# Output projection of the last attention: by token halves of both column tiles between the heads

## The reference, cut to what matters

```python
for blk in range(t // Q_BLOCK):                    # two blocks of 128 queries
    s = einsum('bqhd,bkhd->bhqk', qb, kb) * scale  # 8 heads x 2 sub-heads
    p = softmax(where(allowed, s + bias, -inf))
    attn = p[:, :, 0] - lam_full * p[:, :, 1]
    o = einsum('bhqk,bkhe->bqhe', attn, vb)
    o = o * rsqrt(mean(o * o) + SUBLN_EPS) * subln_g * (1.0 - lambda_init)
h = concatenate(outs, axis=1) @ w_o                # 256 x 1024 by 1024 x 1024
x = layer_norm(ALPHA * x + h, ...)
x = layer_norm(ALPHA * x + square(relu(x @ mlp_w1)) @ mlp_w2, ...)
```

## Time and profile before

| | |
|---|---|
| timed executions, median (lowest to highest) | 1381.98 us (1381.8 to 1383.23) |
| span of the profiled execution | 1382.5 us; the page gives no time for it outside the span |
| PE busy | 1346.9 us, 97% |
| DVE busy | 864.3 us, 63% |
| ACT busy | 673.8 us, 49% |
| stage of the change: from the last k-projection to the MLP's first tile | about 1147 to 1202 us |

### The profile page before, as it was taken

The page is one execution under the profiler, slowest core; times in us unless marked ns, Lnnn a source line. Parts: engine busy times, 40 slices in busy tenths (PEclk is TensorE's granted clock), DMA queues, the critical chain, the costliest instruction groups (busy, mean ns, idle before and its releaser), DMA issues.

```text
span 1382.5 us, 26707 instructions
## 1 busy us (share of the span) xinstructions
PE 1346.9 (97%) x11635; PEld 1195.1 (86%) x11635; DVE 864.3 (63%) x1388; ACT 673.8 (49%) x1202; POOL 87.7 (6%) x104
## 2 busy tenths in 40 slices
PE   8999999999999999999999999999999998999997
PEld 6888998988867889998799999799987896799996
DVE  6786655573395655556685666856467556856565
ACT  6775544552384545442651224445443468545452
POOL 3000400000060000000000430000000000000000
PEclk9999999999999999999999999999999999999999
DMA  9345555453302555554233000655545451555550
GB/s 350 124 182 198 183 183 183 183 198 123 147 38 68 193 189 188 196 191 151 105 140 123 4 5 34 240 200 184 183 183 183 153 183 62 179 193 190 199 184 31
DMA packets 17635, 215.18 MB, mean 156 GB/s; under 512 B 1976, under 2 KB 2144, under 8 KB 4848
## 3 DMA queue, kind: packets, MB, share of 16 engines
q1 hardware_dynamic: 15888, 205.54, 40.3%
q0 software_dynamic: 1632, 7.94, 1.6%
HBM read 212.41 MB, written 1.06 MB: 154 GB/s over the span
## 4 chain that ended last, share of the span: by engine, by line
PE 84%; DVE 9%; ACT 4%; DMA 1%; issue 1%; SPq 0%; DVEq 0%; ACTq 0%
PE psum L665 24%; PE psum L471 11%; PE psum L472 11%; PE psum L473 11%; PE psum L1008 3%; DVE w_low L1862 3%; PE psum L1089 2%; PE psum L569 1%; PE psum L1141 1%; ACT w_high L1342 1%; PE psum L540 1%; PE psum L565 1%; PE psum L541 1%; PE psum L542 1%; DMA ring<-weights 1%; PE psum L561 1%
## 5 line engine op out<-in xcount | busy, mean ns | idle before, releaser
L1862 DVE TENSOR_TENSOR w_low<-ring,w_high 128x1024 fp32r<-128x1024 f32 x368 | 437.0, 1222 | 231.7 <-ACT w_high L1342 231.7
L1342 ACT ACTIVATE w_high<-ring 128x1024 fp32r<-128x1024 f32 x368 | 368.6, 1047 | 175.9 <-PE psum L665 155.4
L471 PE MATMUL psum<-act_split,w_high 128*128 128x256 f32 x1312 | 381.7, 291 | 3.7 <-DVE w_low L1862 3.6
L472 PE MATMUL psum<-act_split,w_high 128*128 128x256 f32 x1312 | 372.5, 284 | 0.0
L473 PE MATMUL psum<-act_split,w_low 128*128 128x256 f32 x1312 | 372.3, 284 | 0.0
L665 PE MATMUL psum<-w_high,up_split 128*128 128x512 f32 x1024 | 287.6, 391 | 0.8 <-DVE up_split L2010 0.8
L471 PEld LDWEIGHTS psum<-act_split,w_high 128*128 128x128 f32 x1312 | 252.6, 193 | 11.6 <-DVE w_low L1862 4.7
L472 PEld LDWEIGHTS psum<-act_split,w_high 128*128 128x128 f32 x1312 | 253.0, 193 | 2.6 <-issue 1.4
L473 PEld LDWEIGHTS psum<-act_split,w_low 128*128 128x128 f32 x1312 | 252.9, 193 | 0.0
L665 PEld LDWEIGHTS psum<-w_high,up_split 128*128 128x128 f32 x1024 | 190.4, 188 | 40.5 <-issue 2.7
L665 PE MATMUL psum<-w_low,up_split 128*128 128x512 f32 x512 | 163.1, 390 | 0.0
(11 more groups left out here) (338 smaller groups left out, 1661.3 us busy)
## 6 DMA issues: line engine op xcount, KB each, us to landing
ring<-weights SPq DMA_DIRECT2D x95, 2048.0 KB, 7.8
work<-rows POOLq DMA_DIRECT2D x4, 1024.0 KB, 5.0
ring<-weights SPq DMA_DIRECT2D x4, 512.0 KB, 8.5
work<-rows POOLq DMA_DIRECT2D x4, 512.0 KB, 5.6
x<-x_in SPq DMA_DIRECT2D x2, 512.0 KB, 4.4
work<-t_bias POOLq DMA_DIRECT2D x1, 1024.0 KB, 8.9
out<-x SPq DMA_DIRECT2D x4, 256.0 KB, 2.0
con<-consts SPq DMA_DIRECT2D x1, 687.0 KB, 21.6
```

Source lines behind the costliest of these rows:

```text
L471: mm(out, w_hi, x_hi, start=start, stop=False)
L472: mm(out, w_hi, x_lo, start=False, stop=False)
L1342: A(high[:, HIGH_SLOT[name], f], ring[:, n % RING, f], ACT.Copy).then_inc(weights_high, 1)
L1862: V.tensor_tensor(low[:, n % RING, f], ring[:, n % RING, f], high[:, HIGH_SLOT[name], f].bitcast(f32), ALU.subtract).then_inc(weights_spli ...
```

## The change: token half 0 of both tiles between the heads

The number of instructions stays the same on every engine; the order changes on PE, and with it the turn list and DVE's order.

- `out_chunk(k, n)` becomes `out_half(k, n, th)`, a half-chunk. Chunks 0 to 3 of tile 0 are still done for both token halves, before the scores of head 7.
- After the scores of head 7 come (k,n,th) = (4,0,0) and (0,1,0) in place of chunk 4 of tile 0; (0,1,0) opens bank 2. After the values of head 6: (5,0,0), (1,1,0), (2,1,0), (3,1,0). After the values of head 7: (4,1,0), (5,1,0), (6,0,0), (4,0,1).
- After the last output transposes: (5,0,1), (6,0,1), (7,0,0), (0,1,1), (1,1,1), (6,1,0), (7,1,0), (7,0,1), then (2,1,1) to (6,1,1), `norm(7, 0)`, (7,1,1).
- Accumulators are filled in the order (0,0), (0,1), (1,0), (1,1); the turn list says so, with the banks unchanged.
- DVE's `norm(7)` loses the `add_in` (1,0) ahead of quarter 0; the existing line `if order[2] == (1, 0)` now does it after quarter 1, ahead of the low parts of token half 0. The other norms keep their order.

```diff
-_mixer_turns(3)
+_norm_turns(7, [(0, 0), (0, 1), (1, 0), (1, 1)], banks={(0, 0): 0, (1, 0): 1, (0, 1): 2, (1, 1): 3})
...
-            out_chunk(4)
+            out_half(4, 0, 0)
+            out_half(0, 1, 0)
             da_transposes(6)
             out_transposes(5)
             da_values(6)
-            out_chunk(5)
-
-            out_chunk(0, 1)
+            out_half(5, 0, 0)
+            out_half(1, 1, 0)
+            out_half(2, 1, 0)
+            out_half(3, 1, 0)
             da_transposes(7)
             out_transposes(6)
             da_values(7)
-            out_chunk(1, 1)
-            out_chunk(6)
+            out_half(4, 1, 0)
+            out_half(5, 1, 0)
+            out_half(6, 0, 0)
+            out_half(4, 0, 1)
             out_transposes(7)
-            out_chunk(2, 1)
-            out_chunk(7)
-            project_out("da_o", 7, act_split, halves=(1,), ks=range(3, NC))
+            out_half(5, 0, 1)
+            out_half(6, 0, 1)
+            out_half(7, 0, 0)
+            out_half(0, 1, 1)
+            out_half(1, 1, 1)
+            out_half(6, 1, 0)
+            out_half(7, 1, 0)
+            out_half(7, 0, 1)
+            for k in range(2, NC):
+                if k == NC - 1:
+                    norm(7, 0)
+                out_half(k, 1, 1)
             mlp(3, 2)
...
                 add_in(i, *order[0])
-                if i % 2:
-                    add_in(i, *order[1])
+                if order[1] == (1, 0):
+                    add_in(i, 1, 0)
                 quarter(0)
```

More of the change, by code:

```diff
@@ L99, with _norm_turns @@
 ACC, TR = {}, {}
-def _norm_turns(i, order, transposes=True):
+def _norm_turns(i, order, transposes=True, banks=None):
     ACC[i], TR[i] = {}, {}
@@ L108, in _norm_turns @@
                 TR[i][(0, n)] = len(BANK) - 1
-        _turns(("acc", i, half), 1, j)
+        _turns(("acc", i, half), 1, banks[half] if banks else j)
         ACC[i][half] = len(BANK) - 1
@@ L1258, in early_heads, with out_half @@
                     da_values(step // 16 - 1)
-            def out_chunk(k, n=0):
+            def out_half(k, n, th):
                 w_hi, w_lo = split_tile(f"da_o{n}")
@@ L1264, in out_chunk @@
                 read_out(pe, TURN[("dot", k)])
[L1265 to L1275, removed]
+                f, t = slice(k * 512, k * 512 + 512), slice(P * th, P * th + P)
+                q = ACC[7][(th, n)]
+                if k == 0:
+                    open_bank(q)
+                for i, (a, w) in enumerate(((0, w_hi), (0, w_lo), (1, w_hi))):
+                    last = mm(bank(q), act_split[:, k, a, t], w[:, f], start=(k == 0 and i == 0),
+                              stop=(k == NC - 1 and i == 2))
+                if k == NC - 1:
+                    last.then_inc(bank_filled, 1)
+            def out_chunk(k):
+                out_half(k, 0, 0)
+                out_half(k, 0, 1)
             project("da_q0", TURN[("da_q", 0)], act_split, beside=beside_queries, second=TURN[("da_q", 1)])
```

## The result

The changed kernel takes 1385.55 us (median of 15 runs, 1383.1 to 1387.25); the kernel before, run beside it 15 times, takes 1383.23 (1380.92 to 1385.18). The ratio is 1.0018, with a 95% interval of 1.0011 to 1.0026: slower by 2.5 us, between 1.5 and 3.6 (the medians themselves are 2.3 apart). The profiled execution of the changed kernel took 1385.41 us with a span of 1383.6, so about 1.8 us lie outside the span.

A forecast was written before the change was run, and what follows sets the result against it. DVE's chain was taken to bound the stage, with PE never pausing behind it. +0.6 (bank 2) + 3.2 (wait for ACT's copy) - 1.68 (closed holes) = +2.1 us on the median 1381.98 gave 1384.1 us, range 1382.0 to 1385.7.

The forecast's parts named there:

- Bank 2, +0.6: After head 7's scores, the half-chunk opening bank 2 waits for DVE's last read: +0.5 and +0.1 us, not absorbed.
- the term of 0.1: At the opening of bank 2, the first matmul after a wait takes 0.34 us to the next instead of 0.23.
- ScalarE's copy starts 12 matmuls later: At the projection's end, the up3_0 copy waits for accumulator (1,0), now filled at the 24th matmul; DVE idles 3.2 us.
- Part 3: End of the projection: ACT's up3_0 copy comes later, and DVE, executing in order, gets 3.2 us of new idle time.
- The holes that close, -1.68: DVE's idle stretches in the stage, 0.24, 1.24 and 0.20 us, close; 1.68 us is the most it can save.
- the sum of +2.1: Whole kernel: +0.6 for bank 2, +3.2 for DVE's wait on ACT's copy, -1.68 for closed holes.
- Parts 2, 4 and 5: Half-chunk swaps between heads cost 0; add_in (1,0) fills DVE's hole after token half 0's norm; down3_0's later load is covered.
- The clock: PE's first idle stretch, 3.3 us, most likely slows the clock off the path; the second, 1.5 us, priced at 0.
- How the numbers follow: Chances for the whole kernel: within 0.2% 0.72, slower by over 0.2% 0.24, faster by over 0.2% 0.04.
- the first rival: Quarter 0 of up3_0 is not late and the holes close: about -0.9 us, 1381.1 us; chance 0.10.
- the third rival: The clock falls in PE's second gap too, ahead of token half 1's transposes: +3.5, 1385.5 us; chance 0.18.
- The second (bank 2 free): Opening bank 2 early costs nothing and the rest stands: +1.5, 1383.5 us; chance 0.12.

The follow-up runs named there:

- e2: The changed kernel with bank 2 opened after the values of head 6 instead of right after the scores of head 7; ratio 1.0006 to the kernel before.
- e1: The changed kernel with VectorE's add_in of accumulator (0,1) ahead of quarter 0 of up3_0 instead of behind it; ratio 1.0013 to the kernel before.
- e4: The changed kernel with bank 2 opened late, accumulators filled (0,0), (1,0), (0,1), (1,1), and VectorE's order as before the change; 1382.1 us, ratio 0.9988.
- e3: The changed kernel with eight idle 128x512 matmuls on TensorE ahead of token half 0's transposes; ratio 1.0018 to the kernel before.
- e5: e4 with token half 1's two low parts ahead of the first two quarters of down3_0 on VectorE; ratio 0.9995 to the kernel before.

## Why the prediction was right or wrong

The mechanism and the size of the sum were right; the step from the sum to the forecast, no change, was wrong.

- *Bank 2, +0.6*: right. 0.60 in the distance from scores to transposes, 0.60 back in the stage of e2. One row was misread on the way: the 0.34 us from 1165.26 to 1165.60, taken for the cost of the first matmul after a wait, stand behind score matmuls and no wait. Behind the real wait of the changed kernel the first matmul took 1166.02 - 1165.71 = 0.31 us to the next, so the term of 0.1 held.
- *ScalarE's copy starts 12 matmuls later and VectorE idles 3.2 us behind (0,0)*: right, 3.15 us. e1 showed that it is the quarter and gave 1.14 us of the delay back. It also showed a second thing on the same hook, the root behind the copies, which Part 3 passed over.
- *The holes that close, -1.68, and the sum of +2.1*: the stage is 1.98 us longer, 0.60 ahead of VectorE's chain and 1.38 on it, where the sum had 0.6 and 3.2 - 1.68 = 1.5. e4 gives the other end of the same account: with both causes out 1.89 us come back against the kernel before, not the 4.5 that TensorE loses there. e3 shows directly that TensorE has room in its first wait.
- *Parts 2, 4 and 5 at nothing*: nothing shows against them. No wait is left ahead of (1,0) or (1,1), ScalarE starts to copy `down3_0` at 1194.83 without a wait, straight behind the norm's root, and TensorE's stretch behind the stage is as busy as before.
- *The clock*: I held a fall in the first gap for most likely and named the gap of 1.56 us as one that did no harm. In the changed kernel's profile it was the other way round: 1.00 after 3.11 us of idling, and 0.50 after the 1.56 us ahead of the last heads. Since the first gap was followed by full speed, TensorE came to the second one earlier and waited 2.37 us there, not 1.5; with a fall, in e2, it waited 0.72. In the stage the fall costs nothing: with the clock falling (e2) or not, the end is where VectorE sets it.
- *Where it failed* is "How the numbers follow". From a sum of +2.1 us it gave 0.72 to "within 0.2%" and 0.24 to "slower", because 0.2% was taken as what a measurement can tell from no change. The ratio is 1.0018 with an interval that ends at 1.0011 on the lower side. The kernel is slower, by less than that bound but clear of no change. The terms of the sum could be traced to rows and only the first rival had the other sign, so the direction, slower by 0.15%, should have been the forecast; calling it no change threw away what the sum said. The other fault there is the base of the absolute number: 1381.98 was the median of three runs, and 15 runs of the same kernel gave 1383.23. Of the 1.45 us between 1384.1 and 1385.55, 1.25 is that, 0.2 the rest. The measured time lies inside the stated range (1382.0 to 1385.7) by 0.15 us, and that is luck: the range reached so far only to take in the third rival, which did not occur.

Rivals: the first (1381.1) and the third (1385.5, the clock falling in the second gap) did not occur: no fall follows the second gap, and the profile of the third would have shown matmuls 0.43 apart there. The third's time lies nearest to the measured one by accident of the base. The second (bank 2 free) is refuted by the wait of 0.38 us.

What stays open: the timed difference is 2.5 us (1.5 to 3.6) and the stage accounts for 1.98. The interval holds it, but single runs of one kernel spread over 4 us and the stage starts anywhere between 1161.95 and 1165.93 us in the seven profiles. Part of that spread goes with TensorE's granted clock. Among the 35 executions of the kernel before that were timed beside e1 to e4, the three with a mean granted clock of 0.994 have a median of 1381.9 us and the eleven with 0.990 one of 1384.18. The profiles have their falls ahead of the stage in different places: e4's, whose stage starts earliest, is the only one without a fall behind the wait of 1.99 us near 81 us. That the falls cause the spread was not tried.

## What to carry to other kernels

When an accumulator is finished earlier or later, list everything that uses its "full" as a signal. Here the same event also freed the slot for the next weight's copy, and the engine that needed the copy had it queued ahead of the sum that had been brought forward. And before one reorders the engine that waits, it pays to add up the work of the engine that it waits for: TensorE lost 4.5 us, but VectorE had only 1.7 us of holes, and that is about what the best order tried gave (1.89).

## What the runs showed of the hardware

- In these profiles the length of an idle stretch did not decide whether the clock fell. Ahead of the transposes of token half 0, TensorE was idle for 2.18 us and the clock fell in the kernel before; after 1.95 us in e1 (0.50 from 1190 to 1192 us) and 3.10 us in e2 it fell; after 3.11 us in the changed kernel it did not.
- The same stretch of instructions, ahead of every edit, came out both ways. TensorE idles for 1.56 us ahead of the last heads in all seven profiles; then follow seven small matmuls and a wait of 0.58 us. The clock stayed at 1.00 before, in e1, e2 and e3, and was at 0.50 behind it in the changed kernel (rows below), in e4 (1149 to 1151 us) and in e5 (1152 to 1154 us). Behind the wait of 1.99 us near 81 us it fell in six profiles and stayed at 1.00 in e4.

```profile
1148.10 0.66 PE L1248 MATMUL psum<-con,work 128*128 128x128 f32 x4 [1.56 <-ACT work L1795]
...
1149.66 0.79 PE L1239 MATMUL psum<-work 128*128 128x128 f32 x2 [0.58 <-ACT work L1778]
...
1150.00:1152.00 2.00, 2.00 (x12) 1.78 (x13) 1.04 (x3) 2.00 (x10) 0.00 (x0) 0.50 1.00 422
```

- The Trainium skill ("TensorE: Matmul & The Clock Gate", section "HAM oscillation — how this bites in real kernels") ties the fall to gaps beyond a certain length. Every gap named here is shorter than that length, and the clock fell behind gaps of 1.95, 2.18 and 3.10 us and behind some of 1.56 and 1.99. That a gap shorter than that length is safe is not borne out by these rows; the measurement decides.
